# Who issues the exchange of the rotary halves, when the rotations run, and how three sink heads' results are split

## The chip, the cores and the metric

One core of one Trainium2 chip runs the kernel. The metric is device time in microseconds (us) of one execution, as the median of several runs; lower is better.

## The reference, cut to what matters

Two transformer blocks follow each other on one sequence of 256 tokens of width 2048, all in float32. The change lies in the second block's attention, which has 8 sink heads over a window (`o_a`) and 8 latent heads (`o_b`). The latent heads' queries are made from a compressed row, and 64 of their 192 features are rotated by position:

```python
def rope(x, positions):
    ...
    x1, x2 = x[..., :half], x[..., half:]
    return jnp.concatenate([x1 * cos - x2 * sin, x2 * cos + x1 * sin], axis=-1)

c_q = rmsnorm_2(proj[..., OFF_MLA_CQ:OFF_MLA_CKV], mla_q_norm_g[l])
q_b = jnp.einsum('bsr,rf->bsf', c_q, w_uq[l]).reshape(B, S, MLA_HEADS, MLA_QK_DIM)
q_rope = rope(q_b[..., MLA_NOPE_DIM:], positions)
kv_b = jnp.einsum('bsr,rf->bsf', c_kv, w_ukv[l])...
o_b = mla_attention(q_nope, q_rope, k_nope, k_rope, v_b)
mix = jnp.concatenate([o_a, o_b], axis=-1)
x = x + g1 * jnp.einsum('bsm,md->bsd', mix, w_out[l])
```

(The sink heads are 16 of 64 features; the kernel handles them in 8 pairs, and a pair is called a head below.)

## The kernel before, in words

Every product with weights runs on TensorE (PE) as a sum of rounded parts: a weight chunk is brought from memory into one of four raw buffers (`RAW`, `NRAW = 4`), ScalarE (ACT, line 1522) copies it to a rounded high part `WHI`, VectorE (DVE, line 1909) subtracts to get the low part `WLO`, and PE multiplies both with the high and low parts of the activations (`HL`: `HI` and `LO`). A chunk is split in one or two parts; four parts can be waiting ahead of PE.

**The order** of everything is written by a planner (`make_plan`). It walks through the slabs of weights chunk by chunk (`run_chunk`), puts the matmuls of each k-tile, a split of a later part after each part, and the evacuation of a slab's result after its last chunk. Other work, attention above all, sits in a list called `side`; `tick` takes a number of steps (`rate`) from it between k-tiles, and an empty entry (`None`) uses up a step. `hook` ties something to a given k-tile of a slab. All engines then walk the same list, each doing its own share of every entry, in order.

**The stretch that matters** comes after the second block's input projection:
- four slabs `uq` (queries, 3 k-tiles of 384 columns each), whose evacuation on ACT (lines 1485 to 1492) writes `qnT` and `qrT` and frees the slab's half of the accumulator (`region`);
- four slabs `ukv` (keys and values, 1 k-tile of 512 columns each), evacuated by ACT into `vb` (line 1498) and then by DVE into `knT` (line 1869), which frees the region;
- the output projection `out2`, whose first two slabs run together, chunk by chunk, with the rest of attention between their k-tiles. Its k-tile k needs the result of head k (`x_ready`): 0 to 7 are the sink heads (numbers 16 to 23 in the program), 8 to 15 the latent heads (24 to 31).

Two slabs are in flight, one in each region, so a slab's first matmul waits for the evacuation of the slab two before it. ACT and DVE take the split of a later part between two evacuations: ACT does the evacuation of `ukv[0]`, the high part of the first half chunk of `out2`, the evacuation of `ukv[1]`, the next high part, and so on, and DVE follows in the same order.

**The rotation.** For each pair of `qrT` slabs the halves of the rotated features must change partitions. The entry `swap` (line 1536) does this with four DMAs of 64 KB into `qsw`, issued on ACT's queue; `rope` (DVE, line 1961) multiplies by cosine and sine and adds, three passes. The scores of latent head h wait for `v_rope` at 2 + h // 4 (line 1188). The entries are tied to k-tiles: `swap 0` to `uq[2]`, `rope 0` to `uq[3]`, `swap 1` to `ukv[0]`, `rope 1` to the second k-tile of `out2[0]`.

**The weights' queue** is SyncE's (SP), `sync_program`, line 2363: for every entry of `P.loads` it waits until the raw buffer's last user (four loads earlier) has been split by ACT and DVE, and issues the next load. Load 330 is `ukv[0]`, loads 331 to 333 the other `ukv`, load 334 the first chunk of `out2[0]`, 335 the first chunk of `out2[4]`'s columns, 336 and 337 their second chunks.

**The heads' results** (entry `out`) leave bank 7 in one of two ways. Either ACT copies the result to `qaT` and a later entry `hsplit` (ACT line 1637, DVE line 2113) makes the high and low parts of several heads at once; or ACT and DVE split it straight from the bank (ACT line 1628, DVE line 2105). Line 687 chooses; for `h5` it takes the second way for the latent heads alone.

Of the kernel before, what the change touches and what calls it, by code (L numbers as in the profile page):

```python
# [78 lines left out]
class Plan:  # L79
# [6 lines left out]
    def slab(self, kind, arg, w, row0, kts, c0, ncol, groups, x, per=None, base=0, cols=None):  # L86
        per = per or max(1, min(8, 2048 // ncol))
        s = dict(tail={("down1z", 12): 1, ("out2", 12): 1, ("down2z", 12): 2}.get((kind, arg), 0), i=len(self.slabs), kind=kind, arg=arg, w=w, row0=row0, kts=kts, c0=c0, nc=ncol,
                 groups=groups, x=x, base=base, cols=cols or slice(c0, c0 + ncol), reg=len(self.slabs) % 2)
        s["list"] = [(s, k, min(per, kts - k), k + per >= kts) for k in range(0, kts, per)]  # L90
        self.slabs.append(s)
        return s
# [33 lines left out]
    def put(self, *unit):  # L126
        self.order.append(unit)
# [15 lines left out]
def make_plan():  # L143
    P = Plan()
    slab, queue, put = P.slab, P.queue, P.put
    w = "nsa_w_in"
# [64 lines left out]
    def uq_columns(j):  # L211
# [5 lines left out]
    uq = [slab("uq", j, "w_uq_2", 0, 3, 0, 384,  # L217
               [("f", 0, 0, 0, S), ("f", 128, 0, 256, S), ("f", 256, 1, 0, S)], "cq", per=3,
               cols=uq_columns(j))
          for j in range(4)]  # L220
    ukv = [slab("ukv", j, "w_ukv_2", 0, 1, 512 * j, 512,
                [("f", 0, 0, 0, S), ("f", 256, 0, 256, S), ("v0", 0, 1, 0, 256), ("v1", 0, 1, 256, 256)], "ckv", per=1)
           for j in range(4)]
    for s in uq + ukv:
        queue(s)
    out2 = down("out2", "w_out_2", 0, KT, "h5", True)
# [42 lines left out]
    side, later, every = deque(), [], []  # L269
    st = dict(split=0, cursor=0, rate=1, due=0.0, parts=0, held=[], kept=0, owing=0, gemv=0.0, credit=0.0)  # L270
# [110 lines left out]
    def hook(s, kx, f, *a):  # L381
        hooks.setdefault((s["i"], kx), []).append((f, a))
# [209 lines left out]
    def run(*ss):  # L592
        for _ in range(sum(len(s["list"]) for s in ss)):
            run_chunk()
# [35 lines left out]
    def hl_free(x, k):  # L630

        return hl_end[x] - (3 - k // 4 if x == "h2" else 0)
# [3 lines left out]
    def flush(x):  # L636
        while got[x] and st["parts"] >= hl_free(x, got[x][0]):
            ks = [got[x].pop(0)]
            while got[x] and len(ks) < 4 and got[x][0] // 4 == ks[0] // 4:
                ks.append(got[x].pop(0))  # L640
            for k in ks:
                P.split_no[x, k] = st["splits"] + 1
            st["splits"] += 1
            if x == "h2":
                P.h2_splits = st["splits"]
            put("hsplit", x, ks[0], len(ks))
            have[x] = ks[-1] + 1
# [4 lines left out]
    def branches(i):  # L652
        return 1 if i >= 24 else 2

    def attention(at, lo, n, last, x):

        for i in range(lo, n + 3 if last else n):
            if i >= 1:
                def s0(i=i):
                    if i - 1 < n and at + i > 1:  # L660
                        put("soft3", at + i - 1)
                    if i >= 2 and i - 2 < n:
                        unit("turn", at + i - 2, 0)
                side.append(s0)

            def s1(i=i):
                if i < n:
                    unit("scores", at + i)
                    put("soft1", at + i)
            side.append(s1)  # L670

            def s2(i=i):
                if 0 <= i - 2 < n and branches(at + i - 2) == 2:
                    unit("turn", at + i - 2, 1)
                if i < n:
                    put("soft2", at + i)
                    if at + i == 0:
                        put("soft3", 0)
            side.append(s2)
            if i >= 3:  # L680
                def s3(i=i):
                    unit("values", at + i - 3)
                    put("out", at + i - 3)
                    k = i - 3
                    if at + k == 31:
                        put("warm", 1)
                    if st["parts"] >= hl_free(x, k) and (x == "h2" or k >= 8):
                        flush(x)
                        st["puts"] += 1
                        P.put_no[at + k] = st["puts"]  # L690
                        have[x] = k + 1
                    else:
                        got[x].append(k)
                side.append(s3)
# [40 lines left out]
    run(sl_cq)  # L735
    run(sl_ckv)
    flush("h5")
    later.append(("latent",))
    hook(uq[2], 1, put, "swap", 0)
    hook(uq[3], 1, put, "rope", 0)  # L740
    hook(ukv[0], 0, put, "swap", 1)
    hook(out2[0], 1, put, "rope", 1)
    run(*uq)
    drain()
    run(*ukv)
# [23 lines left out]
def build(nc, A, out):  # L769
    P = make_plan()  # L770
# [7 lines left out]
    at = [BASE]  # L778
# [111 lines left out]
    qsw = sb("qsw", [128, 4, S], offset=acc_at + 2 * KB)  # L890
# [7 lines left out]
    qrT = un("qrT", [128, 4, S], 56)  # L898
# [23 lines left out]
    l_swap, v_sin = [sem("l_swap0"), sem("l_swap1")], sem("v_sin")  # L922
# [7 lines left out]
    a_u, v_u, a_qfix, v_qfix, a_ufix, v_ufix, v_shift = [sem(n) for n in ("a_u", "v_u", "a_qfix", "v_qfix", "a_ufix", "v_ufix", "v_shift")]  # L930
# [66 lines left out]
    def freed(kind, arg=0):  # L997
        s = name_slab(kind, arg)
        return free_sem[s["free"][0]], s["free"][1]
# [420 lines left out]
    def scalar_program(e):  # L1420
        w = Waits(e)
# [80 lines left out]
        for u in ORDER:  # L1502
            name, *arg = u
            if name == "h1":
                i, = arg
# [4 lines left out]
            elif name == "split" and arg[1] == "hi":  # L1510
                u, _ = arg
                n, a, z = PARTS[u]
# [18 lines left out]
            elif name == "rowsq":  # L1531
                w.wait_ge(l_xrows, 16)
                for h in range(2):
                    w.wait_ge(a_rowsq, h)
                    e.activation(JUNKX[:, :], X[:, h, :], ACT.Square, accum_out=sumx[:, h:h + 1]).then_inc(a_rowsq, 1)
            elif name == "swap":
                i, = arg
                w.wait_ge(*freed("uq", 2 * i + 1))
                w.wait_ge(v_shift, 8)
                for p in range(0, 128, 32):  # L1540
                    e.dma_start(qsw[p:p + 32, 2 * i:2 * i + 2, :], qrT[p ^ 32:(p ^ 32) + 32, 2 * i:2 * i + 2, :]).then_inc(l_swap[i], 16)
            elif name == "cols":
                w.wait_ge(l_crow, 16)
                e.activation(CROW[:, :], CROW[:, :], ACT.Silu).then_inc(a_cact, 1)
# [58 lines left out]
            elif name == "soft2":  # L1603
                i, = arg
# [8 lines left out]
            elif name == "turn":  # L1613
                i, br = arg
# [8 lines left out]
            elif name == "out":  # L1623
                i, = arg
# [7 lines left out]
            elif name == "hsplit":  # L1632
                x, k, n = arg
# [4 lines left out]
            elif name == "usplit":  # L1638
                x, m = arg
# [3 lines left out]
            elif name == "qshift":  # L1643
                i, = arg
# [6 lines left out]
            elif name == "ushift":  # L1651
                s = SLABS[arg[0]]
                i, sa = s["arg"], quarter_of(SA, s["hid"])
# [68 lines left out]
            elif name == "norm":  # L1722
                x, c = arg
# [639 lines left out]
    def sync_program(e):  # L2363
        w = Waits(e)
        for n, (what, index) in enumerate(P.loads):
            for i in XLOAD.get(n, ()):
                a, z = XTILES[i]
                e.dma_start(xT[:, a:z, :], A["x"][:, a:z, :]).then_inc(l_x[i], 16)
            if n >= NRAW:
                before, i = P.loads[n - NRAW]  # L2370
                if before == "w":
                    w.wait_ge(a_hi, part_end[i])
                    w.wait_ge(v_lo, part_end[i])
                elif before == "s":
                    w.wait_ge(v_shift, i + 1)
                else:
                    w.wait_ge(v_mod, 16 * i[0] + i[1] + 1)
            raw = RAW[n % NRAW]
            if what == "w":
                s, k, nk, _ = CHUNKS[index]  # L2380
                cells = nk * s["nc"]
                src, dst = chunk_of(A[s["w"]], P.chunk_at[index], cells), raw[:, 0:cells]
            elif what == "s":
                src, dst = A["w_first"][index], raw[:, :]
            else:
                p, j = index
                src, dst = A["w_mod_2"][16 * p + j], raw[:, :]
            e.dma_start(dst, src).then_inc(l_raw[n % NRAW], 16)
        w.wait_ge(v_store, 1)
        e.dma_start(out_rows[:, 0, 0:512], YROW[:, 0, 0:512]).then_inc(l_out, 16)  # L2390
        w.wait_ge(v_store, 3)
        e.dma_start(out_rows[:, 0, 1024:1536], YROW[:, 0, 1024:1536]).then_inc(l_out, 16)
        w.wait_ge(a_store, 1)
        e.dma_start(out_rows[:, 0, 1536:2048], YROW[:, 0, 1536:2048]).then_inc(l_out, 16)
        w.wait_ge(v_store, 4)
        e.dma_start(out_rows[:, 1, 0:256], YROW[:, 1, 0:256]).then_inc(l_out, 16)
        w.wait_ge(a_store, 2)
        e.dma_start(out_rows[:, 1, 1536:2048], YROW[:, 1, 1536:2048]).then_inc(l_out, 16)
        w.wait_ge(v_store, 6)
        e.dma_start(out_rows[:, 1, 768:1280], YROW[:, 1, 768:1280]).then_inc(l_out, 16)  # L2400
        w.wait_ge(l_table[0], 16)
        w.wait_ge(l_table[1], 16)
        w.wait_ge(l_out, 144)
# [71 lines left out]
```

## Time and profile before

| | |
|---|---|
| median of 3 runs | 2105.72 us (2105.41 to 2106.75) |
| the profiled execution, its own time | 2106.19 us |
| its span, first to last instruction | 2104.4 us |
| mean granted TensorE clock | 0.998 |
| PE busy | 2087.5 us, 99% of the span |
| DVE busy | 1510.9 us, 72% |
| ACT busy | 1059.3 us, 50% |
| DMA of the weights' queue | 488.67 MB, 63.3% of 16 engines' span |

Busy time counts instructions in work; matmuls overlap with the weight loads of the next ones. The issue of a DMA is not counted as busy, though the engine's queue stands still meanwhile. A granted clock of 1.00 is 2.4 GHz, 0.50 is 1.2 GHz. Times in timelines are microseconds from the start of the span.

### The profile page before, as it was taken

The numbers are of one execution on the slowest core, as the hardware profiler recorded it, in microseconds if no ns is written. First come the engines' busy times: TensorE is split into PE (matmuls) and PEld (weight loads), VectorE is DVE, ScalarE is ACT, GpSimd is POOL, SyncE is SP. The second block draws the span as 40 slices with busy tenths as digits, with TensorE's granted clock in tenths as the row PEclk, the third lists the DMA queues.
The fourth block names the chain that finished last, engine by engine and source line by source line (L and its number), as shares of the span: only waits on it lengthen the run. The fifth ranks groups of instructions, "written<-read, shape, count | busy, mean of one in ns | idle before, by whom it ended". The sixth has DMA issues, their size and how long they took to land.

```text
span 2104.4 us, 29119 instructions
## 1 busy us (share of the span) xinstructions
PE 2087.5 (99%) x11332; PEld 1797.1 (85%) x11332; DVE 1510.9 (72%) x2009; ACT 1059.3 (50%) x1534; POOL 18.4 (1%) x34
## 2 busy tenths in 40 slices
PE   9999999999999999999999999999999999999998
PEld 8888888888888888888888898888888888888887
DVE  6869666788989888898766766577555555556555
ACT  6654555554444434444456666565443444344443
POOL 0000000000000000000000000000000000000000
PEclk9999999999999999999999999999999999999999
DMA  8787335788888999988765525455555555555553
GB/s 335 274 309 268 133 101 177 287 317 324 325 330 339 362 368 349 339 328 341 304 250 185 201 87 190 170 215 195 194 188 196 186 198 188 192 193 187 197 183 121
DMA packets 75096, 506.39 MB, mean 241 GB/s; under 512 B 8730, under 2 KB 9226, under 8 KB 17104
## 3 DMA queue, kind: packets, MB, share of 16 engines
q1 hardware_dynamic: 70992, 488.67, 63.3%
q0 software_dynamic: 2864, 14.55, 1.8%
q8 instruction: 91, 1.49, 0.3%
q10 hardware_dynamic: 1104, 1.31, 0.2%
q14 instruction: 45, 0.37, 0.0%
HBM read 501.79 MB, written 2.18 MB: 239 GB/s over the span
## 4 chain that ended last, share of the span: by engine, by line
PE 96%; DVE 2%; ACT 1%; DMA 0%; issue 0%; ACTq 0%; DVEq 0%; SPq 0%
PE region L1156 40%; PE region L1090 30%; PE region L1094 16%; PE region L1145 2%; PE bank L1239 1%; PE bank L1196 1%; PE region L1146 1%; PE bank L1205 1%; PE bank L1129 1%; ACT m_WHI L1522 1%; PE bank L1252 1%; DMA m_RAW<-in_nsa_w_in 0%; PE bank L1182 0%; PE bank L1228 0%; ACT m_SP L1608 0%
## 5 line engine op out<-in xcount | busy, mean ns | idle before, releaser
L1909 DVE TENSOR_TENSOR m_WLO<-m_RAW,m_WHI 128x1024 fp32r<-128x1024 f32 (+3 forms) x729 | 867.7, 1204 | 479.5 <-ACT m_WHI L1522 451.8
L1522 ACT ACTIVATE m_WHI<-m_RAW 128x1024 fp32r<-128x1024 f32 (+3 forms) x729 | 751.8, 1042 | 668.5 <-PE region L1156 311.9
L1156 PE MATMUL region<-m_WHI,m_HL 128*128 128x512 f32 x1152 | 361.3, 395 | 0.5 <-DVE m_HL L2113 0.5
L1090 PE MATMUL region<-m_HL,m_WHI 128*128 128x512 f32 x1472 | 357.4, 393 | 0.0
L1090 PE MATMUL region<-m_H,m_WHI 128*128 128x512 f32 x1376 | 328.7, 391 | 0.0
L1090 PEld LDWEIGHTS region<-m_HL,m_WHI 128*128 128x128 f32 x1472 | 269.5, 188 | 52.1 <-issue 0.3
L1090 PEld LDWEIGHTS region<-m_H,m_WHI 128*128 128x128 f32 x1376 | 252.8, 188 | 48.9
L1156 PEld LDWEIGHTS region<-m_WHI,m_HL 128*128 128x128 f32 x1152 | 212.8, 188 | 43.2 <-issue 1.4
L1945 DVE CUSTOM_DVE_ANT_0 m_RAW<-m_RAW,m_CROW,m_consts 128x2048 f32<-128x2048 f32 x96 | 225.2, 2345 | 0.2 <-DMA m_RAW<-in_w_mod 0.2
L1156 PE MATMUL region<-m_WLO,m_HL 128*128 128x512 f32 x576 | 224.6, 390 | 0.0
L1156 PE MATMUL region<-m_WHI,m_HIDL 128*128 128x512 f32 (+1 forms) x512 | 198.3, 387 | 0.0
L1156 PE MATMUL region<-m_WLO,m_HIDH 128*128 128x512 f32 (+1 forms) x512 | 198.3, 387 | 0.0
L1156 PE MATMUL region<-m_WHI,m_HIDH 128*128 128x512 f32 (+1 forms) x512 | 198.3, 387 | 0.0
L1094 PE MATMUL region<-m_HL,m_WLO 128*128 128x256 f32 x1472 | 195.5, 284 | 0.2 <-DVE m_HL L2270 0.2
L1094 PEld LDWEIGHTS region<-m_HL,m_WLO 128*128 128x128 f32 x1472 | 188.6, 191 | 8.0 <-issue 1.4
L1094 PEld LDWEIGHTS region<-m_H,m_WLO 128*128 128x128 f32 x1376 | 176.4, 191 | 6.7
L1094 PE MATMUL region<-m_H,m_WLO 128*128 128x256 f32 x1376 | 178.5, 283 | 0.0
L1156 PEld LDWEIGHTS region<-m_WLO,m_HL 128*128 128x128 f32 x576 | 108.1, 188 | 23.0
L1156 PEld LDWEIGHTS region<-m_WHI,m_HIDL 128*128 128x128 f32 x512 | 96.1, 188 | 19.9
L1156 PEld LDWEIGHTS region<-m_WHI,m_HIDH 128*128 128x128 f32 x512 | 96.1, 188 | 19.7
L1156 PEld LDWEIGHTS region<-m_WLO,m_HIDH 128*128 128x128 f32 x512 | 96.1, 188 | 19.5
L1145 PE MATMUL region<-m_HL,m_WHI 128*128 128x512 f32 x192 | 68.3, 399 | 1.2 <-DVE m_WLO L1909 0.8
(335 smaller groups left out, 1749.4 us busy)
## 6 DMA issues: line engine op xcount, KB each, us to landing
m_RAW<-in_w_ff SPq DMA_DIRECT2D x124, 1024.0 KB, 4.8
m_RAW<-in_w_mod SPq DMA_DIRECT2D x96, 1024.0 KB, 6.6
m_RAW<-in_ffn_w_in SPq DMA_DIRECT2D x88, 1024.0 KB, 6.4
m_RAW<-in_ffn_w_out SPq DMA_DIRECT2D x44, 1024.0 KB, 6.7
m_RAW<-in_nsa_w_in SPq DMA_DIRECT2D x36, 1024.0 KB, 5.8
m_RAW<-in_nsa_w_out SPq DMA_DIRECT2D x16, 1024.0 KB, 4.9
m_RAW<-in_w_out SPq DMA_DIRECT2D x16, 1024.0 KB, 5.0
m_RAW<-in_w_first SPq DMA_DIRECT2D x8, 1024.0 KB, 4.9
```

The costliest lines, as they stand in the source:

```text
L1090: mm = e.matmul(region[s["reg"]][:, b, :], hi[:, i, c:c + 128], both[:, k + a + i, :, :].rearrange("p a s -> p (a s)"), start=k + a + i == ...
L1094: mm = e.matmul(region[s["reg"]][:, b, 0:S], lo[:, i, c:c + 128], xh, start=False, stop=stop, skip_group_check=True)
L1129: mm = e.matmul(bank[4][0:120, 0:256], ZHL[s["arg"]][:, kx, :, :].rearrange("p a s -> p (a s)"), wv, start=start and i == 0, stop=fin and ...
L1145: e.matmul(o, wh[:, c:c + 128], both, start=start, stop=fin, skip_group_check=True)
L1146: mm = e.matmul(o[:, 0:S], wl[:, c:c + 128], xh, start=False, stop=fin, skip_group_check=True)
L1156: mm = e.matmul(o, lhs, rhs, start=start and i == 0, stop=fin and i == 2, skip_group_check=True)
L1196: mm = e.matmul(bk[:, o:o + n], lhs, rhs, start=j == 0, stop=j == len(pr) - 1, skip_group_check=True)
L1205: tp = e.transpose(bank[6][:, dst:dst + 128], sp[:, src:src + 128], ident[:, :])
L1239: ins = e.matmul(dst, lhs, rhs, start=j == 0, stop=j == len(mm) - 1, skip_group_check=True)
L1522: e.activation(WHI[u % 4][:, 0:(z - a) * ncol], raw[:, a * ncol:z * ncol], ACT.Copy).then_inc(a_hi, 1)
L1909: e.tensor_tensor(WLO[u % 4][:, 0:m], raw[:, a * ncol:z * ncol], WHI[u % 4][:, 0:m].bitcast(F32), ALU.subtract).then_inc(v_lo, 1)
L1945: e.tensor_tensor_reduce(out=raw[:, :], in0=raw[:, :], in1=CROW[:, :], scale=1.0, scalar=bmod[:, c:c + 1], op0=ALU.mult, op1=ALU.add, accu ...
```

## The change

It does three things. The four DMAs of each exchange are issued by SP: the planner notes at which load (`P.swap_at`, the number of loads listed so far) an exchange stands, and SP, when it comes to that load, first waits for the queries' evacuation, issues the four DMAs, and goes on to the load; these places are load 330 (`hook(uq[2], 1, ...)`) and load 334 (`hook(ukv[0], 0, ...)`). Both rotations are entries of the side list around the scores of head 24, in `out2[0]`, with two empty steps between. The condition `k >= 8` on line 687 goes, so that heads 21 to 23 are split straight from the bank.

```diff
@@ attention
-            side.append(s1)
+            if at + i == 24:
+                side.extend([lambda: put("rope", 0), None, None, s1, lambda: put("rope", 1)])
+            else:
+                side.append(s1)
@@ s3
-                    if st["parts"] >= hl_free(x, k) and (x == "h2" or k >= 8):
+                    if st["parts"] >= hl_free(x, k):
@@ make_plan
+    def exchange(i):
+        P.swap_at[len(P.loads)] = i
+
+    P.swap_at = {}
     later.append(("latent",))
-    hook(uq[2], 1, put, "swap", 0)
-    hook(uq[3], 1, put, "rope", 0)
-    hook(ukv[0], 0, put, "swap", 1)
-    hook(out2[0], 1, put, "rope", 1)
+    hook(uq[2], 1, exchange, 0)
+    hook(ukv[0], 0, exchange, 1)
@@ scalar_program
-            elif name == "swap":
-                i, = arg
-                w.wait_ge(*freed("uq", 2 * i + 1))
-                w.wait_ge(v_shift, 8)
-                for p in range(0, 128, 32):
-                    e.dma_start(qsw[p:p + 32, 2 * i:2 * i + 2, :], qrT[p ^ 32:(p ^ 32) + 32, 2 * i:2 * i + 2, :]).then_inc(l_swap[i], 16)
@@ sync_program
+            if n in P.swap_at:
+                pair = P.swap_at[n]
+                own = slice(2 * pair, 2 * pair + 2)
+                w.wait_ge(*freed("uq", 2 * pair + 1))
+                w.wait_ge(v_shift, 8)
+                for p in range(0, 128, 32):
+                    e.dma_start(qsw[p:p + 32, own, :], qrT[p ^ 32:(p ^ 32) + 32, own, :]).then_inc(l_swap[pair], 16)
             if n >= NRAW:
                 before, i = P.loads[n - NRAW]
```

## Rows read from the trace of the kernel before

**Rows 1.** The page, busy time of each engine, its share and instructions.

```profile
PE 2087.5 (99%) x11332; PEld 1797.1 (85%) x11332; DVE 1510.9 (72%) x2009; ACT 1059.3 (50%) x1534; POOL 18.4 (1%) x34
```

**Rows 2.** Waits of PE, 1240 to 1345 us: releaser, us in total, times, longest.

```profile
PE region L1156 <- ACT m_WHI L1522: 2.5, 1, 2.5
PE region L1156 <- DVE m_HL L2113: 0.5, 1, 0.5
```

**Rows 3.** Timeline of PE: start, us, line, operation, [idle before it <- releaser].

```profile
1267.83 0.28 PE L1156 MATMUL region<-m_WLO,m_CQH 128*128 128x256 f32 x1
1270.66 0.36 PE L1156 MATMUL region<-m_CQH,m_WHI 128*128 128x256 f32 x1 [2.55 <-ACT m_WHI L1522]
...
1271.17 0.41 PE L1156 MATMUL region<-m_CQH,m_WHI 128*128 128x256 f32 x1
...
1275.18 0.69 PE L1156 MATMUL region<-m_WHI,m_HL 128*128 128x512 f32 x2
```

**Rows 4.** Windows: stretch, length, busy time per engine, PEclk, DMA share, GB/s.

```profile
1268.00:1270.60 2.60, 0.11 (x1) 0.00 (x0) 1.58 (x3) 1.75 (x4) 0.00 (x0) 1.00 0.83 261
1270.60:1274.30 3.70, 3.64 (x18) 3.67 (x19) 2.99 (x4) 2.55 (x6) 0.00 (x0) 0.55 1.01 343
```

**Rows 5.** Timeline of ACT and its DMA queue (ACTq), 1258 to 1271 us.

```profile
1258.79 0.60 ACT L1489 ACTIVATE m_qnT<-region 128x512 f32<-128x512 f32 x1 [0.17 <-PE region L1156]
1259.29 0.38 ACT L1492 ACTIVATE m_qrT<-region 128x256 f32<-128x256 f32 x1
...
1259.69 3.27 ACTq L1541 DMA_DIRECT2D m_qsw<-m_qrT  x4
1263.06 0.63 ACT L1522 ACTIVATE m_WHI<-m_RAW 128x512 fp32r<-128x512 f32 x1 [2.99 <-issue]
...
1264.34 1.15 ACT L1522 ACTIVATE m_WHI<-m_RAW 128x512 fp32r<-128x512 f32 x2
...
1265.86 0.39 ACT L1492 ACTIVATE m_qrT<-region 128x256 f32<-128x256 f32 x1
...
1266.28 2.45 ACTq L1541 DMA_DIRECT2D m_qsw<-m_qrT  x4
1268.85 0.84 ACT L1498 ACTIVATE m_vb<-region,m_rstdl 128x256 f32<-128x256 f32 x2 [2.08 <-PE region L1156]
1269.58 1.06 ACT L1522 ACTIVATE m_WHI<-m_RAW 128x1024 fp32r<-128x1024 f32 x1
```

**Rows 6.** Timeline of DVE, 1265 to 1280 us.

```profile
1265.67 0.68 DVE L1967 TENSOR_TENSOR m_ropeQ<-m_qrT,m_cosT 128x512 f32<-128x512 f32 x1
...
1269.82 0.69 DVE L1869 TENSOR_TENSOR m_knT<-region,m_rstd 128x512 f32<-128x512 f32 x1 [0.94 <-ACT m_vb L1498]
1270.74 1.23 DVE L1909 TENSOR_TENSOR m_WLO<-m_RAW,m_WHI 128x1024 fp32r<-128x1024 f32 x1 [0.23 <-ACT m_WHI L1522]
...
1279.14 1.01 DVE L2098 TENSOR_SCALAR m_SP<-m_SP,m_stat 128x256 f32<-128x256 f32 x4
```

**Rows 7.** Timeline of SP's DMA queue: start of the first, us to the last's end.

```profile
2.12 0.91 SPq L2388 DMA_DIRECT2D m_RAW<-in_nsa_w_in  x2
...
1246.87 14.20 SPq L2388 DMA_DIRECT2D m_RAW<-in_w_ukv  x4
1264.55 79.21 SPq L2388 DMA_DIRECT2D m_RAW<-in_w_out  x13
```

**Rows 8.** DMA issues: KB each, us to landing; `ukv`, then loads 334 and 335.

```profile
m_RAW<-in_w_ukv SPq DMA_DIRECT2D x4, 256.0 KB, 2.7
...
m_RAW<-in_w_out SPq DMA_DIRECT2D x1, 1024.0 KB, 4.8
...
m_RAW<-in_w_out SPq DMA_DIRECT2D x1, 1024.0 KB, 8.8
```

**Rows 9.** Timeline of DVE and PE around the split of heads 21 to 23.

```profile
1299.78 0.96 DVE L2113 TENSOR_TENSOR m_HL<-m_qaT,m_HL 128x768 fp32r<-128x768 f32 x1 [0.38 <-ACT m_HL L1637]
...
1300.89 0.70 PE L1156 MATMUL region<-m_WHI,m_HL 128*128 128x512 f32 x2 [0.49 <-DVE m_HL L2113]
```

## The prediction

> **What bounds the kernel now.** I read the page's busy times first: PE is in work 99% of the span [rows 1], so the time is PE's work plus PE's pauses plus whatever the clock takes. The change adds and removes no matmul; it can only move the pauses. The waits of PE in the second block's attention come next, and there are just two [rows 2]: 2.5 us that the view puts down to ACT's high part, and 0.5 us for the low parts of heads 21 to 23.
>
> The timeline shows where the first one is from [rows 3]. PE ends `ukv[1]` at 1268.11 and starts `ukv[2]` at 1270.66, 2.55 us later. Its weights are split by then; what it needs is its region, freed by the `knT` pass of `ukv[0]`. That pass ran from 1269.82 to 1270.51 [rows 6], and it followed ACT's `vb` copies, which started only at 1268.85 since ACT's queue had been issuing the second exchange since 1266.28, 2.45 us for four DMAs [rows 5]. So the pause belongs to the exchange, and the releaser named in the view merely ended last. The first exchange held ACT 2.99 us as well (1263.06, "issue" [rows 5]), and no PE wait stands beside it.
>
> The pause costs more than itself. From 1270.6 to 1274.3 the granted clock averages 0.55 [rows 4]: PE ran mostly at 1.2 GHz after 2.55 us without work, and a matmul took 0.41 us in place of 0.28 [rows 3]. That is 0.45 x 3.70 = 1.7 us of full-clock work lost. Removing the ACT stall is worth at most 2.55 + 1.7 = 4.25 us, with the heads' 0.49 [rows 9] some 4.7.
>
> **Part 1, ACT freed of eight DMA issues.** By itself this would take those 4.25 us. It holds only if what ACT does next is there when ACT comes: high parts of loads 330 and 334.
>
> **Part 2, SP burdened with them.** What stands behind the new waits on SP is the weights. Before, SP issued the four `ukv` loads from 1246.87 to 1261 and load 334 at 1264.55 [rows 7]. Now load 330 stands behind `uq[1]`'s evacuation (over at 1259.29 + 0.38 = 1259.67 [rows 5]) and four issues. No row shows an exchange issued by SP. ACT's cost 2.45/4 = 0.61 each in the quieter case and 3.27/4 = 0.82 in the other [rows 5]; SP's own issues back to back are 0.91/2 = 0.46 [rows 7]. I take 0.61, the same descriptors without a rival issuer, and keep 0.46 and 0.82 as ends.
> - First exchange: 1259.75 + 2.4 = 1262.2; load 330 lands 2.7 later [rows 8], 1264.9. ACT, whose next item is this high part, waits from 1260.1 (before: until 1263.06), and behind it stand `uq[2]`'s and `uq[3]`'s evacuations. High part 0.63, evacuation 1258.79 to 1259.67 = 0.88, two high parts 1.15, evacuation 0.88 [rows 5]; with the 0.1 by which neighbours overlap, `uq[2]` is out at 1266.35 and `uq[3]` at 1268.2, against 1266.25 before. PE pauses some 1.4 us before `ukv[0]` and 0.4 before `ukv[1]`.
> - Second exchange: SP waits for `uq[3]`, 1268.25, issues until 1270.7, then load 334 goes, 6.1 us later than before. Issued 1.3 us ahead of the next, it took 4.8 to land [rows 8]: 1275.5 against 1269.35. ACT reached this item at 1269.58 before [rows 5], so 334 was just in time and has no slack to give.
> - From 1275.5: high part 1.06 [rows 5], low part 1.23, `knT` of `ukv[1]` 0.69 [rows 6], with 0.1 between engines 1278.5; PE starts `ukv[3]` at 1278.7. The next low part 1.23, then `knT` of `ukv[2]` 0.69: 1280.3, and PE starts `out2` at 1280.4. Before, it did so at 1275.18 [rows 3]. **+5.2 us.** The same walk over the order of before gives 1274.8 without the slow clock; it reproduces the trace within half a microsecond.
>
> 1275.18 already holds the 1.7 us of slow clock, and 1280.4 doesn't. PE now pauses nearly 7 us before `ukv[3]`, more than the 2.55 that preceded the fall, so I charge one such stretch again, on `ukv[3]` and the start of `out2`: **+1.7 us** (ends 0 and 3.4).
>
> A rule of the Trainium skill bears on this part (DMA: Bandwidth & Descriptors, section "Issuing engines are not separate DMA queues"): the engine that issues a transfer changes only the sequencer time of the issue, usually small beside the transfer. Read alone, it would make the move a plain gain of ACT's issue time, about 4.7 us less with clock and heads; the trace disagrees with "small" (2.45 us here [rows 5]), and my sum is about something the rule leaves out, the wait ahead of the loads.
>
> **Part 3, rotation 0 moves.** Three passes of 0.68 [rows 6] leave the `uq` stretch, where DVE waits for ACT anyway: nothing gained once ACT is late. They now stand in `out2` after head 23's last softmax step (1.4 us with its small operations, the bulk the 1.01 of [rows 6]). Head 24's scores wait for them. DVE, ending the last low part at 1283.4, would be through at 1286.8; PE has three k-tiles and a turn of about 4.7 us to do from 1280.4, to 1285.1 at full clock and 1286.8 with the slow stretch. I take 0 and keep 1.6 as the upper end. Rotation 1 was in this place already. The four extra steps delay the rest of attention by two k-tiles; the last head then ends in `out2`'s third round of chunks, before its k-tile comes.
>
> **Part 4, heads 21 to 23.** One ACT and one DVE pass over 768 columns go and three short DVE passes come, an engine that idles in this stretch. The 0.49 us wait [rows 9] goes, since k-tile 5 needs head 21 alone: **-0.5 us**. If another wait takes its place, 0.
>
> **The sum:** +5.2 + 1.7 - 0.5 = +6.4 us on the profiled execution's 2106.19, its span being 2104.4; it lies 0.47 over the median, so the median moves from 2105.72 to 2112.1. Ends: issues at 0.46 or 0.82 each, -1.2 or +1.6; clock -1.7 or +1.7; rotation +1.6. If four weight loads issued within 1.4 us share the DMA engines, 334 may take up to 335's 8.8 us [rows 8], +4.0.
>
> **The rivals.** A difference within 0.2% (4.2 us) is about what can't be told from no change here.
> - *The load is in time (faster).* Place: ACT's high part of load 334. Price: the pause and slow clock go, -4.7, giving 2101.0. It decides if 334 lands by about 1269.6. Counting back 4.8 us, SP would have to issue it by 1264.8, while `uq[3]` is evacuated at 1266.25 at best [rows 5] and four issues follow. For it: only that my reading of SP's order could be wrong. 8%. This is also where the Trainium skill's rule quoted in part 2 (DMA: Bandwidth & Descriptors, "Issuing engines are not separate DMA queues") would lead.
> - *Late, but cheaply (within 0.2%).* Issues at 0.46, a quicker landing, no extra slow clock: +5.2 - 1.2 - 0.5 = +3.5, 2109.2. 14%. Another 1% that the parts cancel at 2105.7: that would need the exchange to stand at other loads than 330 and 334.
> - *Late and contended (slower still).* 334 shares the engines, or rotation 0 and a second slow stretch add: +6.4 + 4 to 5, 2117. Against it: one queue's loads seem served in order, 4.8 for the first and 8.8 for the second. 10%.
> - *The forecast*, 2112.1: 67%.
>
> The numbers follow: slower by over 0.2% is 67 + 10 = 77%, within 15%, faster 8%. The range leaves out the fast rival and the outer part of the contended one: 2108.5 to 2117.0.
>
> Another rule, same page, section "Rules for kernel authors", asks to issue a DMA early and wait late; the change does the opposite to four weight loads, and the trace agrees that it matters, ACT having needed 334 0.2 us after it landed.
>
> **What would show it.** In SP's queue the first `ukv` load near 1262 and the first `out2` load near 1270.7; ACT's high part at 1275.5 waiting for a DMA; a PE pause of 6 to 7 us before `ukv[3]` and short ones before `ukv[0]` to `ukv[2]`; `out2` starting near 1280 to 1282; granted clock near 0.5 for some 3.4 us there; no wait for line 2113. I'd be wrong if load 334 went out before 1266, or if `out2` began before 1275.

## The result and the profile after

The changed kernel takes 2115.08 us (median of 5 runs, 2114.58 to 2116.21), the kernel before 2105.92 us in the same session (5 runs, 2105.41 to 2108.24). The ratio is 1.0043, 95% interval 1.0029 to 1.0057: slower by 9.2 us, the interval being 6 to 12 us. The profiled execution took 2114.59 us with a span of 2112.8, 8.4 us longer than the span before.

The lines of `kernel.py` moved: before's 1156 (matmul), 1522 (high part), 1909 (low part), 1869 (`knT`) are 1161, 1527, 1908 and 1868 now; the exchange is line 2374, the weights' load 2394.

The page, busy times, beside [rows 1]:

```profile
PE 2089.1 (99%) x11332; PEld 1798.2 (85%) x11332; DVE 1511.5 (72%) x2011; ACT 1060.1 (50%) x1533; POOL 18.4 (1%) x34
```

As many matmuls, with PE busy 1.6 us longer on the same work. The waits of PE from 1230 to 1360 us, beside [rows 2] (columns as there):

```profile
PE region L1161 <- DVE m_knT L1868: 7.2, 2, 6.8
PE region L1161 <- DVE m_WLO L1908: 2.2, 2, 2.0
PE bank L1201 <- DVE m_qrT L1970: 1.4, 1, 1.4
```

10.8 us in place of 3.0. The queue that issues the weights and now the exchanges (start of the first, us to the end of the last), beside [rows 7]:

```profile
1259.26 3.11 SPq L2374 DMA_DIRECT2D m_qsw<-m_qrT  x4
1262.47 1.98 SPq L2394 DMA_DIRECT2D m_RAW<-in_w_ukv  x4
1268.58 2.41 SPq L2374 DMA_DIRECT2D m_qsw<-m_qrT  x4
1271.09 87.63 SPq L2394 DMA_DIRECT2D m_RAW<-in_w_out  x14
```

All four `ukv` loads stand behind the first exchange, and load 334 behind the second: it goes at 1271.09, not 1264.55. ACT's timeline, beside [rows 5]:

```profile
1258.85 0.38 ACT L1497 ACTIVATE m_qrT<-region 128x256 f32<-128x256 f32 x1
...
1265.17 0.63 ACT L1527 ACTIVATE m_WHI<-m_RAW 128x512 fp32r<-128x512 f32 x1 [5.54 <-DMA m_RAW<-in_w_ukv]
...
1276.07 1.06 ACT L1527 ACTIVATE m_WHI<-m_RAW 128x1024 fp32r<-128x1024 f32 x1 [6.26 <-DMA m_RAW<-in_w_out]
1277.03 0.82 ACT L1503 ACTIVATE m_vb<-region,m_rstdl 128x256 f32<-128x256 f32 x2
```

ACT no longer stands still to issue DMAs; it waits 5.54 and 6.26 us for the loads instead, with the evacuations behind. DVE follows, beside [rows 6]:

```profile
1277.22 1.23 DVE L1908 TENSOR_TENSOR m_WLO<-m_RAW,m_WHI 128x1024 fp32r<-128x1024 f32 x1 [6.60 <-ACT m_WHI L1527]
1278.37 0.68 DVE L1868 TENSOR_TENSOR m_knT<-region,m_rstd 128x512 f32<-128x512 f32 x1
...
1280.10 0.68 DVE L1868 TENSOR_TENSOR m_knT<-region,m_rstd 128x512 f32<-128x512 f32 x1
...
1287.74 0.69 DVE L1970 TENSOR_TENSOR m_qrT<-m_ropeQ,m_qsw 128x512 f32<-128x512 f32 x1
```

And PE, beside [rows 3]:

```profile
1266.82 0.36 PE L1161 MATMUL region<-m_CQH,m_WHI 128*128 128x256 f32 x1 [2.02 <-DVE m_WLO L1908]
...
1279.20 0.55 PE L1161 MATMUL region<-m_CQH,m_WHI 128*128 128x256 f32 x1 [6.76 <-DVE m_knT L1868]
...
1281.89 1.05 PE L1161 MATMUL region<-m_WHI,m_HL 128*128 128x512 f32 x2
...
1288.58 0.46 PE L1201 MATMUL bank<-m_knT,m_qnT 128*128 128x128 f32 x2 [1.44 <-DVE m_qrT L1970]
```

The `knT` pass that ends at 1279.05 frees the region for the fourth `ukv` slab at 1279.20. `out2` begins at 1281.89. At head 24's scores PE waits 1.44 us for rotation 0, which ends at 1288.43. The windows over the long pause and the work behind it, beside [rows 4]:

```profile
1272.40:1279.20 6.80, 0.04 (x2) 0.03 (x1) 1.98 (x3) 3.13 (x6) 0.00 (x0) 0.79 0.96 390
1279.20:1283.20 4.00, 4.00 (x16) 3.71 (x17) 2.84 (x4) 2.34 (x5) 0.00 (x0) 0.50 1.04 428
```

Four microseconds of matmuls ran at 1.2 GHz, 2.0 us of full-clock work, where before it was 1.7. What this costs in time is less, as experiment 1 shows. The clock had fallen inside the pause already: over its 6.80 us it averages 0.79.

**Where the time went.** At `uq[1]`'s evacuation this trace is 0.44 us ahead of the one before (1258.85 against 1259.29). From there to the start of `out2` it takes 1281.89 - 1275.18 + 0.44 = 7.15 us more, slow clock included; +1.44 for rotation 0, -0.49 for the heads: +8.1 of the 8.4 us. The slow clock behind the start of `out2` (1.4 us of matmuls) is not in this sum.

### The profile page after: what moved, and what is told of

It is laid out like the page before. It is cut to its first block, busy times and chain, and to the rows that moved or that the text cites. A ratio compares the mean times of both kernels' runs of the same rounds, so it can differ in the third digit from the quotient of the medians.

```text
span 2112.8 us, 29118 instructions
## 1 busy us (share of the span) xinstructions
PE 2089.1 (99%) x11332; PEld 1798.2 (85%) x11332; DVE 1511.5 (72%) x2011; ACT 1060.1 (50%) x1533; POOL 18.4 (1%) x34
## 4 chain that ended last, share of the span: by engine, by line
PE 95%; DVE 2%; ACT 1%; DMA 1%; issue 0%; SPq 0%; DVEq 0%; ACTq 0%
PE region L1161 40%; PE region L1095 30%; PE region L1099 15%; PE region L1150 2%; PE bank L1244 1%; PE bank L1201 1%; PE region L1151 1%; PE bank L1210 1%; PE bank L1134 1%; PE bank L1257 1%; ACT m_WHI L1527 1%; DMA m_RAW<-in_nsa_w_in 1%; DVE m_WLO L1908 0%; PE bank L1187 0%; PE bank L1233 0%
```

## The experiments

The theory was that the loads behind the exchanges are the loss, rotation 0 a small one, the heads a small gain. The main rivals were the moved rotations as the loss, and exchanges that cost on this queue wherever they stand. Ratios are to the kernel before, run beside each group on the same chip; its medians were 2106.51, 2106.49 and 2105.95 in the three groups. Intervals are some ±0.09% (±1.8 us), for the changed kernel and experiment 3 ±0.14%; for the difference of two experiments I estimate ±0.13% (±2.7 us), √2 times the first. Experiments 5 to 8 ran on another chip than the others. No kernel leaves out any of the computation.

### 1. Heads alone

Against the kernel before:

```diff
-                    if st["parts"] >= hl_free(x, k) and (x == "h2" or k >= 8):
+                    if st["parts"] >= hl_free(x, k):
```

> The kernel before with the condition on the heads alone changed: heads 21 to 23 are split straight from the bank. Theory: the 0.49 us wait of PE for the low parts of heads 21 to 23 goes and nothing else moves, 0.5 us less than before (about 2105.4 against 2105.9), the 2.55 us pause before the third ukv slab and its 3.4 us of slow clock stay. Rival (the direct split holds bank 7 longer and delays a later head): a new PE wait in the output projection, no gain or up to 1 us more.

Measured: 2105.57 us, ratio 0.9997 (0.9988 to 1.0006). PE's waits, 1240 to 1400 us:

```profile
PE region L1156 <- ACT m_WHI L1522: 3.0, 1, 3.0
PE bank L1252 <- DVE m_X L1807: 0.8, 2, 0.6
PE region L1156 <- DVE m_knT L1869: 0.4, 1, 0.4
```

The wait for the low parts of the heads is gone, and no wait for bank 7 has come (the second line stands in the kernel before too, with 0.5). In time this is too small to be told from nothing. One expectation failed: the slow clock did not stay. The windows of the pause and the work behind it:

```profile
1268.20:1271.20 3.00, 0.03 (x2) 0.04 (x1) 0.76 (x2) 1.82 (x4) 0.00 (x0) 1.00 0.80 291
1271.20:1275.00 3.80, 3.32 (x24) 2.94 (x24) 3.73 (x5) 3.50 (x7) 0.00 (x0) 1.00 1.02 327
```

A pause of 2.98 us, longer than the 2.55 of the kernel before, and the granted clock stays at 1.00. So this trace prices the slow clock. From the first matmul of `ukv[2]` to the first of `out2`:

```profile
1271.19 0.35 PE L1156 MATMUL region<-m_CQH,m_WHI 128*128 128x256 f32 x1 [2.98 <-ACT m_WHI L1522]
...
1275.05 0.70 PE L1156 MATMUL region<-m_WHI,m_HL 128*128 128x512 f32 x2
```

That is 3.86 us at full clock (3.85 in experiment 2), where the kernel before takes 1275.18 - 1270.66 = 4.52 [rows 3]. The slow clock cost 0.66 us there and not 1.7: at full clock PE stands idle between these matmuls (busy 3.32 of 3.80 us, with one wait of 0.39 for `knT`), so that most of the 1.7 falls into time that PE would have spent waiting.

### 2. ACT issues again, rotations and heads as changed

Against the changed kernel:

```diff
-    hook(uq[2], 1, exchange, 0)
-    hook(ukv[0], 0, exchange, 1)
+    hook(uq[2], 1, put, "swap", 0)
+    hook(ukv[0], 0, put, "swap", 1)
```

and the issue moved from `sync_program` back to `scalar_program`.

> The changed kernel with the two exchanges issued by ACT again, at their old places; rotations and heads as changed. Theory (the loss is made by the weight loads behind the exchanges on SP): load 334 goes out near 1264.5 and lands near 1269.4 again, the pauses are 2.55 us before the third ukv slab as in the kernel before, and about 2 us at head 24's scores, where rotation 0 is no longer done early; 0.49 us less for the heads. Sum +1.5, about 2107.4. Rival (the moved rotations and the attention pushed back by two k-tiles are the loss, the queue is incidental): close to the changed kernel, 2112 to 2115.

Measured: 2108.60 us, ratio 1.0011 (1.0002 to 1.0019), +2.3 us where +1.5 was expected. The two longest of PE's waits:

```profile
PE region L1161 <- ACT m_WHI L1527: 2.9, 1, 2.9
PE bank L1201 <- DVE m_qrT L1976: 1.7, 1, 1.7
```

Of the change's 0.43% this part holds 0.11%. The old pause is back (2.89 us, with no slow clock behind it), and PE waits 1.66 us for rotation 0 in its new place.

### 3. SP issues, rotations and heads as before

Against the kernel before:

```diff
-    hook(uq[2], 1, put, "swap", 0)
+    hook(uq[2], 1, exchange, 0)
-    hook(ukv[0], 0, put, "swap", 1)
+    hook(ukv[0], 0, exchange, 1)
```

and the issue moved from `scalar_program` to `sync_program`, as in the change.

> The kernel before with the exchanges issued by SP before loads 330 and 334 alone; rotations and heads as before. Theory: load 334 goes out near 1271 and lands near 1276, PE pauses over 6 us before the fourth ukv slab, the slow clock returns, no wait of 1.4 us at head 24's scores, the 0.49 us for heads 21 to 23 stays: changed kernel's 2115.1 less 1.4 plus 0.5, about 2114.1. Rival (the moved rotations are the loss): within 1 us of 2105.9, or below it by up to 4.2 since ACT is free.

Measured: 2114.13 us, ratio 1.0035 (1.0022 to 1.0049), the 2114.1 that was expected. The profiled execution is the longest of the five, 2116.84 us. SP's queue, then the three longest of PE's waits:

```profile
1270.16 2.43 SPq L2373 DMA_DIRECT2D m_qsw<-m_qrT  x4
1272.69 26.20 SPq L2393 DMA_DIRECT2D m_RAW<-in_w_out  x7
```

```profile
PE region L1160 <- DVE m_knT L1867: 7.9, 2, 6.5
PE region L1160 <- DVE m_WLO L1907: 2.0, 1, 2.0
PE region L1160 <- DVE m_HL L2111: 0.5, 1, 0.5
```

The queue alone makes some four fifths of the loss (0.35% of 0.43%, each ±0.14%). The rotations as the main cause are out.

### 4. Both exchanges behind loads 334 to 337

Against the changed kernel:

```diff
-    P.swap_at = {}
+    P.swap_at = {338: (0, 1)}
-    hook(uq[2], 1, exchange, 0)
-    hook(ukv[0], 0, exchange, 1)
-            if n in P.swap_at:
-                pair = P.swap_at[n]
+            for pair in P.swap_at.get(n, ()):
```

> The changed kernel with both exchanges issued by SP just before load 338, behind loads 334 to 337, in place of before 330 and 334. Theory: the ukv loads and load 334 go out as in the kernel before, no pause before a ukv slab above 0.5 us and no slow clock (-4.2), heads -0.5, and a wait at head 24's scores of 2 us, or up to 4 if the exchanges land late beside four 1 MB loads: 2103 to 2105. Rival (an exchange on the weights' queue costs wherever it stands, since its small packets slow the loads): loads 334 to 337 land later by 2 us or more and the time stays above 2108.

Measured: 2109.10 us, ratio 1.0008 (1.0000 to 1.0017), runs from 2104.46 to 2111.26. The median is the rival's (above 2108), its mechanism is not: the `ukv` pauses are 0.41 and 0.69 us, near the theory's 0.5, and the 1 MB loads of the stretch land after 8.2 us (median), no later than in the kernel before (9.1). What the theory had too small is the wait at head 24's scores and, behind it, a slow clock that it had put at nothing (0.57 on average from 1283.00 to 1286.80). The exchange was late for rotation 0, by 1.48 us. DVE's timeline, then PE's wait:

```profile
1279.94 0.69 DVE L1963 TENSOR_TENSOR m_qsw<-m_qsw,m_sinT 128x512 f32<-128x512 f32 x1 [1.48 <-DMA m_qsw<-m_qrT]
```

```profile
PE bank L1196 <- DVE m_qrT L1965: 3.2, 1, 3.2
```

So the long pause goes when load 334 no longer stands behind an exchange. And a DMA of 64 KB, which landed after 1.9 to 2.8 us in the changed kernel, took 7.1 to 9.2 here beside four loads of 1 MB. How much of the 3.2 us is this late landing and how much is the rotation's place is what experiment 8 asks.

### 5. Exchanges between loads that nobody needs soon, rotation 0 before the last `ukv` evacuation

Against the changed kernel, with the loop of experiment 4:

```diff
-    P.swap_at = {}
+    P.swap_at = {336: (0,), 338: (1,)}
-    hook(uq[2], 1, exchange, 0)
-    hook(ukv[0], 0, exchange, 1)
+    hook(ukv[3], 0, put, "rope", 0)
-                side.extend([lambda: put("rope", 0), None, None, s1, lambda: put("rope", 1)])
+                side.extend([None, None, None, s1, lambda: put("rope", 1)])
```

> Exchange 0 issued by SP before load 336, exchange 1 before load 338 (no load that ACT is about to need stands behind them), rotation 0 just before the last ukv slab's evacuation on DVE, rotation 1 after head 24's scores, heads 21 to 23 from the bank. Theory: loads 330 to 335 go out as in the kernel before; PE's pauses of the stretch are the 1.1 us (0.4 and 0.7) that the run with both exchanges before load 338 showed, without its 3.2 us at head 24's scores, no slow clock: 1.9 us less than before by the pauses, up to 3.6 with the slow clock, so about 2102.6 to 2104.3. Rival (exchanges on this queue cost wherever they stand): 2107 or more, with loads 334 and 335 landing over 2 us later or a new pause.

Measured: 2103.56 us (2102.23 to 2105.77, 11 runs), ratio 0.9987 (0.9978 to 0.9996). It beats both kernels: 2.7 us less than before (interval 0.8 to 4.6), some 11.8 less than the changed one by the two ratios. SP's queue and PE's waits:

```profile
1264.29 2.10 SPq L2389 DMA_DIRECT2D m_RAW<-in_w_out  x2
1266.44 2.49 SPq L2369 DMA_DIRECT2D m_qsw<-m_qrT  x4
1269.03 1.67 SPq L2389 DMA_DIRECT2D m_RAW<-in_w_out  x2
1270.75 2.41 SPq L2369 DMA_DIRECT2D m_qsw<-m_qrT  x4
```

```profile
PE region L1157 <- ACT m_WHI L1523: 0.4, 1, 0.4
PE region L1157 <- DVE m_knT L1864: 0.4, 1, 0.4
```

The same eight issues on the same queue, now with no load behind them that PE is about to wait for: 0.8 us of pauses in the stretch where the kernel before has 3.0 and the changed one 10.8. The rival (this queue is dear wherever the exchange stands) is out.

### 6 and 7. One old place at a time

Against experiment 5:

```diff
-    P.swap_at = {336: (0,), 338: (1,)}
+    P.swap_at = {330: (0,), 338: (1,)}
```

in experiment 6, and in experiment 7:

```diff
-    P.swap_at = {336: (0,), 338: (1,)}
+    P.swap_at = {334: (1,), 336: (0,)}
```

> As the run with the exchanges before loads 336 and 338, but exchange 0 before load 330, its place in the changed kernel. It prices the first exchange's place. Theory: ACT waits for the first ukv load until about 1265, pauses of 2 us before the first ukv slab and some tenths before the next two; load 334, no longer held by an exchange but by the late split of load 330, lands 2 to 3 us late: 3 to 5 us over that run, without the 6 us pause. Rival (load 334's place alone matters): within 1 us of that run.

> As the run with the exchanges before loads 336 and 338, but exchange 1 before load 334, its place in the changed kernel. It prices the second exchange's place. Theory: load 334 goes out near 1268.8 instead of 1263.5 and lands 5 us late; a pause of 4 to 5 us before the fourth ukv slab and a slow clock behind it: 5 to 7 us over that run, so that the two places together (with the run on load 330) give the changed kernel's loss and the second is the larger. Rival (the first exchange starts the loss): under 2 us over that run.

Measured: 2107.95 us, ratio 1.0011 (1.0002 to 1.0020), and 2110.95 us, ratio 1.0021 (1.0012 to 1.0030). PE's waits of experiment 6, then of 7:

```profile
PE region L1157 <- DVE m_WLO L1904: 2.8, 1, 2.8
PE region L1157 <- DVE m_knT L1864: 1.6, 1, 1.6
```

```profile
PE region L1157 <- DVE m_knT L1864: 7.2, 2, 6.8
```

Over experiment 5, load 330's place costs 0.24% (5 us) and load 334's 0.34% (7 us); together 12, where the whole change stands 0.56% (11.8 us) over experiment 5, its 1.4 us for rotation 0 included. Both places cost, as expected, the second more. Together in one kernel they cost 9 us with the rotation's place taken out (experiment 8), so 12 and 9 are no different within the noise, and whether the two prices add is not shown.

### 8. Rotation 0 back in the first output slab

Against experiment 5:

```diff
-    hook(ukv[3], 0, put, "rope", 0)
-                side.extend([None, None, None, s1, lambda: put("rope", 1)])
+                side.extend([lambda: put("rope", 0), None, None, s1, lambda: put("rope", 1)])
```

> As the run with the exchanges before loads 336 and 338, but rotation 0 in the first output slab as in the changed kernel, after head 23's last softmax step. Theory: the exchange has landed by then, DVE's three passes and the low part before them come too late for head 24's scores: one pause of 1.4 to 2 us there (1.44 in the changed kernel, 1.66 with ACT issuing), 1.4 to 2 us over that run. Rival (the 3.2 us wait seen with both exchanges before load 338 is the place's own price, not the late landing): 3 us over it.

Measured: 2106.38 us, ratio 1.0000 (0.9991 to 1.0009), 0.13% (2.8 us) over experiment 5, runs from 2104.59 to 2110.61. The profiled execution is the longest of these runs and shows this, ACT's timeline and then PE's:

```profile
1274.47 1.06 ACT L1522 ACTIVATE m_WHI<-m_RAW 128x1024 fp32r<-128x1024 f32 x1 [2.30 <-DMA m_RAW<-in_w_out]
```

```profile
1281.99 0.77 PE L1196 MATMUL bank<-m_knT,m_qnT 128*128 128x128 f32 x2 [3.63 <-DVE m_qrT L1965]
```

The exchange had landed; ACT and DVE were late with load 335's parts, which stand ahead of rotation 0, and PE was early. The place costs 2.8 us by the medians, where the theory had 1.4 to 2 and the rival 3: the rival is closer, which speaks for experiment 4's wait being mostly the place's price and not the late landing's. Its price is how far DVE is behind PE when `out2` begins, 1.4 to 3.6 us in four traces.

This kernel also gives the cleanest price of the exchanges' places, since it differs from the changed kernel in these alone: 1.0043 against 1.0000, 0.43% or 9 us (an interval of some ±3.5 us, estimated from the two).

### 9 and 10. The wait and the issues by themselves

Against experiment 5, for experiment 9:

```diff
+            if n == 334:
+                w.wait_ge(*freed("uq", 3))
```

and for experiment 10:

```diff
-    P.swap_at = {336: (0,), 338: (1,)}
+    P.swap_at = {334: (0,), 338: (1,)}
```

> As the run with the exchanges before loads 336 and 338, with SP made to wait for the evacuation of the last query slab before load 334, and no DMA issued there. It prices the wait without the issues. Theory: in the traces that wait ends 1.3 to 1.6 us after load 334 would have gone (1265.6 against 1264.3), so 334 is late by that much and ACT's high part with it: 1 to 1.6 us over that run, 2104.6 to 2105.2, with a pause of 1.4 to 2 us before the fourth ukv slab. Rival (only what is transferred ahead of the load counts): no difference.

> As the run with the exchanges before loads 336 and 338, but exchange 0 before load 334: its data have been ready for 4 us there, so this prices the four issues without a wait. Theory: 334 is late by the four issues, 2.5 us: 2 to 2.5 us over that run, about 2105.6 to 2106.1, or up to 1.7 more where the slow clock follows the pause. With the run on the wait this makes up the 5 us or more of exchange 1 before load 334. Rival (the issues are cheap on SP, the wait is everything): within 0.7 us of that run.

Measured: the wait 2108.36 us, ratio 1.0009 (1.0000 to 1.0018); the issues 2105.21 us, ratio 0.9996 (0.9987 to 1.0005). SP's queue and ACT's timeline of 9, then the same of 10:

```profile
1266.22 0.80 SPq L2391 DMA_DIRECT2D m_RAW<-in_w_out  x2
```

```profile
1271.06 1.06 ACT L1523 ACTIVATE m_WHI<-m_RAW 128x1024 fp32r<-128x1024 f32 x1 [3.46 <-DMA m_RAW<-in_w_out]
```

```profile
1262.17 3.23 SPq L2369 DMA_DIRECT2D m_qsw<-m_qrT  x4
1265.50 3.39 SPq L2389 DMA_DIRECT2D m_RAW<-in_w_out  x4
```

```profile
1270.51 1.06 ACT L1523 ACTIVATE m_WHI<-m_RAW 128x1024 fp32r<-128x1024 f32 x1 [1.91 <-DMA m_RAW<-in_w_out]
```

The issues cost 0.09% (1.9 us) over experiment 5, as expected, though by times alone this is not clear of nothing (±2.7 us). The wait costs 0.22% (4.6 us), three times what was expected. Between the two, run side by side, lie 3.2 us, and of 22 runs the shortest with the wait (2107.13) and the longest with the issues (2107.23) barely overlap.

The error was in the expectation: it set 1265.6 of one trace against 1264.3 of another, though these traces are 2 us apart in that stretch (their `ukv` loads begin at 1253.25 and 1255.54). Set against `uq[3]`'s evacuation in the same trace (1267.93 in experiment 5, 1266.20 in 9, 1267.20 in 10), load 334 goes 3.6 us ahead of it, at its end, and 1.7 us ahead of it. So the wait delays the load by 3.7 us, the issues by 1.9, and the price in time follows: 4.6 and 1.9, against 7 for both in experiment 7. The slow clock is a part of the 4.6, how large is not shown: behind 9's pause of 3.95 us, 6.1 us of matmuls ran at 1.2 GHz, behind 10's of 2.40 the clock stayed at 1.00.

## Why the prediction was right

The forecast was 2112.1 us, slower, in a range of 2108.5 to 2117.0; measured 2115.08. Step by step:

- **ACT freed by itself is worth up to 4.25 us, if the loads are there.** Experiment 5 shows that condition: with the loads in time it is 2.7 us less than before, the heads in it. The traces account for it: PE's pauses fall from 3.0 to 0.8 us, and the slow clock gives back 0.7 (experiment 1), 2.9 in all. The upper end of 4.25 was too high, above all since it took the slow clock at 1.7.
- **First exchange on SP.** Issues until 1262.2 and ACT at its high part at 1264.95 predicted, 1262.37 and 1265.17 measured. The first four issues took 3.11 us, 0.78 each, nearer to the upper end (0.82) than to the 0.61 taken; SP began 0.5 us earlier, so it came out even. PE paused 2.02 us where I had 1.4 before `ukv[0]`.
- **Second exchange on SP.** 0.60 per issue against 0.61; load 334 at 1271.09 against 1270.7, ACT's high part at 1276.07 against 1275.5, `ukv[3]` at 1279.20 against 1278.7, `out2` at 1281.89 against 1280.4 + 1.7 = 1282.1. Lined up at `uq[1]`'s evacuation, where this trace is 0.44 us ahead, each measured time is 0.44 later: 7.15 us more to the start of `out2`, where +5.2 and +1.7 were predicted.
- **The slow clock.** That it would return was right. Its size in time was not: 1.7 is the work lost, and before it cost 0.66 us (experiment 1). The recorded walk shows this too, for 1274.8 without the slow clock against 1275.18 with it leaves 0.4, not 1.7. In the changed kernel it cost 0.9 us up to `out2` (1281.89 - 1279.20 = 2.69, against 1275.05 - 1273.25 = 1.80 for the same matmuls at full clock in experiment 1) and at most 0.7 behind it. Without it `out2` would have begun at about 1281.0, an estimate on this trace's own clock, where the walk had 1280.4. So the walk was 0.6 us short and the clock 0.8 too dear, and that the two met at 1282 is luck.
- **Rotation 0** was taken at 0 with 1.6 as the end: 1.44 measured, 1.66 with ACT issuing, 2.8 by the medians with everything else mended. Of the terms of the sum this is the mis-sized one that shows in the total. I let the slow clock bring PE as late as DVE; DVE was later still, its last low part ending at 1285.2 instead of 1283.4, because the evacuation of `ukv[3]` before it waits for PE.
- **Heads 21 to 23:** the wait is gone, -0.49 in the trace, below what the runs can tell.
- **The sum** on the profiled execution: +6.4 predicted, +8.4 measured, of which rotation 0 makes 1.44. The medians lie 9.2 apart, with an interval of 6 to 12.

The rival that ended faster needed load 334 on its way before 1264.8; it went at 1271.09. The rule that led there (the Trainium skill, DMA: Bandwidth & Descriptors, section "Issuing engines are not separate DMA queues") speaks of the sequencer's issue time alone, and in these runs four issues are 2.4 to 3.6 us of a queue's time on either engine. My remark that the trace disagrees with "small" took four issues together and set no transfer beside them: in the changed kernel one issue took 0.6 us in the median, beside 1.9 to 2.8 us from issue to landing. What decides is what else stands in that queue: the same eight issues are 9 us dearer at loads 330 and 334 than at 336 and 338 (experiment 8), 11.8 with rotation 0's later place.

The same page of the Trainium skill (DMA: Bandwidth & Descriptors, section "Rules for kernel authors") asks for early issue and a late wait. Here it holds for the weights, with numbers: in the kernel before load 334 landed 0.2 us before its use, and in experiment 9 3.7 us of delay from a wait ahead of it became 4.6 us of time.

## What to carry to other kernels

A DMA moved to an idle-looking queue takes its waits along: list what stands behind it there, how long ahead of use each of those is issued, and place it behind the last load that somebody is about to need. The wait in front of the moved DMA cost more than its issues here (4.6 against 1.9 us). When a pass moves to a later place, ask how far its engine lags behind the one that waits, at that place, and line up traces by a common event before subtracting their times. Price a slow clock by the time between two such events and not by the work lost (0.66 us against 1.7 here).

## What was not expected of the hardware

- **The same pause, two clocks.** The kernel before paused 2.55 us and the clock fell to 1.2 GHz behind it; experiment 1 paused 2.98 and experiment 2 2.89, at the same place, and the granted clock stayed at 1.00. In experiment 6, with 2.75 before `ukv[0]`, it fell. In these traces 2.5 to 3 us without work can go either way, so a saving of that sort is 0 or some 0.7 us in one execution. Behind pauses of 6.8 us two traces differ as well: 4.0 us of matmuls at 1.2 GHz in the changed kernel, 5.8 in experiment 7:

```profile
1276.40:1282.20 5.80, 5.73 (x22) 5.07 (x22) 5.76 (x8) 3.13 (x6) 0.00 (x0) 0.50 1.02 371
```

What decides it was not tried.
- **Issues of one form differ.** Four issues of an exchange took 2.41 to 3.60 us on SP and 2.45 to 3.27 on ACT. It is one issue that is long: in the changed kernel the eight took 0.59 us in the median and one of them 1.21, in experiment 6 one took 1.70, and where all four are short they make 2.4 to 2.5. It isn't the first exchange as such, since in experiment 1 ACT took 2.53 for the first and 2.98 for the second. Nor does it need a rival issuer, as I had supposed: in the changed kernel no other engine issues a DMA during the 3.11 us. Its cause is open.
